# One-hot tiles for 256 tokens: two broadcast compares and a GpSimd multiply, or eight scalar compares per four tokens

## The reference

```python
def peer(h, w_q, sub_k1, sub_k2, u, v):
    ...
    sc, pos = lax.top_k(cand, PEER_TOPK)                 # 16 experts for each of 8 heads
    eidx = jnp.take_along_axis(cidx, pos, axis=-1)       # expert number = i1 * 128 + i2
    gate = jax.nn.softmax(sc, axis=-1)
    ...
        act = jax.nn.gelu(jnp.einsum('td,thkd->thk', hx, u[ex]))
        return jnp.einsum('thk,thkd->td', (gx.astype(act.dtype) * act), v[ex])
```

## Time and profile before

| | |
|---|---|
| median of 3 runs | 1987.02 us (1985.88 to 1988.28) |
| the profiled execution, device time | 1985.47 us |
| its span, first to last instruction | 1983.6 us |
| busy: TensorE, its weight loads | 1738.9 us (88%), 1106.4 us (56%) |
| busy: VectorE | 1137.5 us (57%) |
| busy: ScalarE | 244.2 us (12%) |
| busy: GpSimd | 694.1 us (35%) |
| mean granted TensorE clock | 0.934 of full |
| DMA | 475.53 MB, mean 240 GB/s |

### The profile page before, as it was taken

One profiled execution on the slowest core, in us unless ns is written; L12 is line 12 of the kernel. 1 busy time (PEld: TensorE's weight loads), 2 busy tenths in 40 slices (PEclk: granted clock), 3 DMA queues, 4 the chain that ended last, 5 costly groups with the idle time before them and its releaser, 6 DMA issues.

```text
span 1983.6 us, 17251 instructions
## 1 busy us (share of the span) xinstructions
PE 1738.9 (88%) x6170; PEld 1106.4 (56%) x6170; DVE 1137.5 (57%) x2433; ACT 244.2 (12%) x601; POOL 694.1 (35%) x714
## 2 busy tenths in 40 slices
PE   6979899999999899999999993768999999995067
PEld 3454344333678588888888882655444444442033
DVE  0011233333120999999974568999565555668933
ACT  2002232233011102111111110000000000000023
POOL 0001133333000233333443446776444333546700
PEclk9979899999999999999999996778999999998589
DMA  5231110100544579999998997114999999999911
GB/s 199 74 117 54 32 33 21 30 2 2 189 139 149 191 280 339 367 370 362 364 384 323 409 409 288 58 53 172 409 409 409 409 409 409 409 409 404 409 49 43
DMA packets 131969, 475.53 MB, mean 240 GB/s; under 512 B 14715, under 2 KB 15739, under 8 KB 131884
## 3 DMA queue, kind: packets, MB, share of 16 engines
q0 software_dynamic: 73728, 268.47, 35.1%
q1 hardware_dynamic: 58156, 205.97, 28.1%
HBM read 471.19 MB, written 3.19 MB: 239 GB/s over the span
## 4 chain that ended last, share of the span: by engine, by line
PE 55%; DMA 27%; DVE 9%; POOL 4%; issue 4%; ACT 1%; SPq 0%; DVEq 0%; ACTq 0%; POOLq 0%
DMA arena<-in_v,eidx 19%; PE psum L1366 16%; DMA arena<-in_u,eidx 7%; PE psum L1215 6%; PE psum L1277 6%; PE psum L1113 5%; POOL arena L477 4%; PE psum L1193 3%; PE psum L1237 3%; PE psum L1326 3%; PE psum L1249 3%; PE psum L1377 3%; PE psum L1165 2%; DVE arena L973 2%; DVE arena L951 2%
## 5 line engine op out<-in xcount | busy, mean ns | idle before, releaser
L1366 PE MATMUL psum<-arena 128*128 128x256 f32 x2048 | 442.5, 379 | 0.7 <-ACT arena L589 0.7
L1384 PE MATMUL psum<-arena 128*128 128x512 f32 x1024 | 440.4, 592 | 2.8 <-DMA arena<-in_vd 2.0
L477 POOL DMA_INDIRECT arena<-in_u,eidx x256 | 246.9, 964 | 518.2 <-DVE dots L951 293.3
L973 DVE SCALAR_TENSOR_TENSOR arena<-arena,wts 128x1024 f32<-128x1024 f32 x254 | 325.7, 1285 | 169.6 <-DMA arena<-in_v,eidx 169.5
L1366 PEld LDWEIGHTS psum<-arena 128*128 128x128 f32 x2048 | 389.0, 190 | 53.7 <-ACT arena L589 0.9
L951 DVE CUSTOM_DVE_ANT_0 arena<-psum,arena 128x1024 f32<-128x1024 f32 x256 | 304.0, 1222 | 64.4 <-DMA arena<-in_u,eidx 62.3
L477 POOL DMA_INDIRECT arena<-in_v,eidx x256 | 249.8, 976 | 253.7 <-DVE arena L973 219.5
L1384 PEld LDWEIGHTS psum<-arena 128*128 128x128 f32 x1024 | 194.2, 190 | 247.7 <-issue 243.0
L458 POOL TENSOR_SCALAR arena<-arena 128x256 f32<-128x256 f32 (+4 forms) x128 | 105.9, 846 | 375.6 <-DVE arena L747 245.1
L1377 PE MATMUL psum<-arena 128*128 128x128 f32 x512 | 103.2, 366 | 71.5 <-POOL arena L487 28.9
L1377 PEld LDWEIGHTS psum<-arena 128*128 128x128 f32 x512 | 90.5, 266 | 84.5 <-issue 43.4
(11 more groups left out here) (167 smaller groups left out, 1348.3 us busy)
## 6 DMA issues: line engine op xcount, KB each, us to landing
arena<-in_ut SPq DMA_DIRECT2D x128, 512.0 KB, 6.8
arena<-in_vd SPq DMA_DIRECT2D x128, 512.0 KB, 6.8
arena<-in_wpack SPq DMA_DIRECT2D x105, 512.0 KB, 3.7
arena<-in_u,eidx POOLq DMA_INDIRECT x256, 8.9
arena<-in_v,eidx POOLq DMA_INDIRECT x256, 14.7
arena<-in_w_pg SPq DMA_DIRECT2D x8, 512.0 KB, 8.9
arena<-in_x SPq DMA_DIRECT2D x4, 512.0 KB, 4.8
arena<-bias_rows SPq DMA_DIRECT2D x8, 256.0 KB, 5.4
```

The source lines that it names most:

```text
L477: G.indirect_dma_start(out=slots[n % SLOTS], out_offset=None, in_=a["v"] if values else a["u"], in_offset=bass.IndirectOffsetOnAxis(ap=eid ...
L973: V.scalar_tensor_tensor(to, row, w, to, ALU.mult, ALU.add).then_inc(row_used, 1)
L1366: last = T.matmul(ps[6 + c % 2][:, 0:DT], u[:, k * P:(k + 1) * P], h2T1[:, k, :], start=(k == 0), stop=(k == KC - 1))
L1384: last = T.matmul(ps[BANK + 2 * t + h], mixed[:, c, t * P:(t + 1) * P], stream[:, c % SRING, h * HALF:(h + 1) * HALF], start=(c == 0), sto ...
```

## The change

`make_hots` makes each token's one-hot by itself, with tensor_scalar instructions of 128x128: `iota` is compared with a per-partition scalar, a column of `pickT`. For `hot2` a second operation of the same instruction multiplies by the gate, a second per-partition scalar. Four such instructions are made for `hot2` and four for `hot1`, and the semaphore goes up with the last of each four. The multiply on GpSimd, its two waits and the semaphore `hot2_gated` are gone; GpSimd's gathers stay in their order. TensorE waits for `hot2_ready`.

```diff
@@ gpsimd
             for n in range(before):
                 gather(n)
-            pool.wait_ge(picks_out, 2)
             for g in range(WG):
-                pool.wait_ge(hot2_ready, g + 1)
-                G.tensor_tensor(hot2[:, g % 2, :, :], hot2[:, g % 2, :, :],
-                                pickT[:, 2, WGRP * g:WGRP * (g + 1)].unsqueeze(2).broadcast_to([P, WGRP, P]),
-                                ALU.mult).then_inc(hot2_gated, 1)
                 if g % W_STEP == W_STEP - 1 and g // W_STEP >= 1:
                     gather(before + g // W_STEP - 1)
@@ vector
             def make_hots(g):
                 if g >= 2:
                     dve.wait_ge(mix_made, g - 1)
-                V.tensor_tensor(hot2[:, g % 2, :, :], iota[:, :].unsqueeze(1).broadcast_to([P, WGRP, P]),
-                                pickT[:, 1, WGRP * g:WGRP * (g + 1)].unsqueeze(2).broadcast_to([P, WGRP, P]),
-                                ALU.is_equal).then_inc(hot2_ready, 1)
-                V.tensor_tensor(hot1[:, g % 2, :, :], iota[:, :].unsqueeze(1).broadcast_to([P, WGRP, P]),
-                                pickT[:, 0, WGRP * g:WGRP * (g + 1)].unsqueeze(2).broadcast_to([P, WGRP, P]),
-                                ALU.is_equal).then_inc(hot1_ready, 1)
+                for j in range(WGRP):
+                    tok = WGRP * g + j
+                    last = V.tensor_scalar(hot2[:, g % 2, j, :], iota[:, :], pickT[:, 1, tok:tok + 1],
+                                           pickT[:, 2, tok:tok + 1], ALU.is_equal, ALU.mult)
+                last.then_inc(hot2_ready, 1)
+                for j in range(WGRP):
+                    tok = WGRP * g + j
+                    last = V.tensor_scalar(hot1[:, g % 2, j, :], iota[:, :], pickT[:, 0, tok:tok + 1], None, ALU.is_equal)
+                last.then_inc(hot1_ready, 1)
@@ tensor
             for g in range(WG):
                 pe.wait_ge(hot1_ready, g + 1)
-                pe.wait_ge(hot2_gated, g + 1)
+                pe.wait_ge(hot2_ready, g + 1)
```

More of the change, by code:

```diff
@@ L299, in build @@
         hot2_ready = sem("hot2_ready")
-        hot2_gated = sem("hot2_gated")
         mix_made = sem("mix_made")
```

## The result

The changed kernel takes 2008.53 us (median of 3 runs, 2003.60 to 2012.12) against 1987.02 before: +21.5 us between the medians. The ratio of the runs on record is 1.0099, with a 95% interval of 1.0069 to 1.0129. It is slower, as forecast, by over three times what I forecast (+6.4). The number lies within 0.1 us of the first rival's, the second scalar that costs as much as the first (2008.6).

The account below looks back on a forecast made before the run. VectorE was taken to bound the one-hot stage: 140.3 + 18.2 = 158.5 us against 152.1, so +6.4. With everything behind the stage unchanged, 1987.0 + 6.4 = 1993.4 us; range 1988 to 2013.

Parts of the forecast that it names:

- first rival: hot2 instructions in the one-hot stage: second fetched scalar costs another 0.06 us, 0.259 each; +21.6 us, 2008.6; chance 0.27.
- What bounds the stage: Loop over 64 four-token groups, 152.1 us: VectorE sets the pace, TensorE close behind; mean period 2.38 us.
- the 133.4 us of VectorE: Stage before the change: VectorE's need if nothing held it, 64 x (0.60 + 0.60 + 0.60) + 16 x 1.14.
- The coupling: DMA-bound stretch behind the stage stays as long: a microsecond of the stage is a microsecond of the end.
- Part (a): GpSimd's 64 multiplies go, and with them the hold on L1006 (7 us) and late matmuls (up to 9.6 us).
- Part (c): Eight tensor_scalar of 128x128 per group at 0.199 us each, second scalar free: 1.59 us per group against 1.20.
- the slow rate: Sign in the changed trace that comparing isn't done at two elements per step: starts 0.26 us apart.
- Part (e): TensorE in the stage: matmuls take at most 2.06 us plus 0.3, within 2.79 us, so VectorE's waits for them vanish.
- the case that I had given 0.42: The forecast itself: second scalar's fetch costs nothing more, stage 158.5 us, +6.4 us, time 1993.4 us.
- The hidden fetch: One-hot instructions: fetch hidden when short, 0.139 us each; TensorE last, stage 134 us, -18, time 1969; chance 0.13.
- the slow comparison: One-hot instructions: is_equal not at two elements per step, 0.266 us each; +41 us, 2028, or 2043; chance 0.07.
- A lock for a gather's whole length: Stage's 16 GpSimd gathers each stop VectorE for 0.94 us: 15 us on top of the forecast, 2008.5; chance 0.05.

Follow-up runs that it names:

- per-token version: Kernel before with the gate multiply moved from GpSimd to ScalarE and a semaphore raised for each token: 2039.21 us beside 2054.80 for the kernel before, on a disturbed chip.
- half change: Changed kernel with hot1 made by the one broadcast comparison of before, hot2 still by four tensor_scalar: 2006.96 us, ratio 1.0098; later 2071.16 and 2066.52 us on disturbed chips.

## Why the prediction was right or wrong

**What bounds the stage** held. VectorE's instructions from start to start give the length of every stage, and without the multiply the 133.4 us of VectorE became 135.0.

**The coupling** held in all kernels: the rest is 611.9 to 614.4 us for stages of 128 to 174 us, begun anywhere from 1217 to 1293. Where the stage began on time, its difference is the kernel's. For the change that is 174.4 - 152.1 = +22.3 of a span that grew by 23.1; it began 2.4 us later and its rest was 1.6 shorter.

**Part (a)**, what GpSimd's leaving gives, held: 7 + 9.6 reckoned, 17.1 measured.

**Part (c)** held for the first scalar: 0.199 us reckoned, 0.197 measured, at two elements per step with is_equal as well. It failed at the second scalar. I gave it the lower end, nothing, "the two come from one row of the same tile, and nothing in the rows says that the fetch is longer than its latency". The measured term is 0.06 us on each of 256 instructions, 15.4 us, beside a miss of 15.1 (2008.5 against 1993.4). The stage without it was 16.5 us shorter, since the 1.5 us beside the gathers went with it. Nothing in the rows spoke for the overlap either. They showed that not even the next instruction's start hides a fetch, and the nearest priced thing to a second fetch was the first. The hot2 starts of 0.256 us also look like the 0.26 that I had named as the sign of the slow rate. It is not that: the hot1 starts are at 0.197, and with no fetch the same comparison and multiply take 0.136.

**Part (e)** held: 0.5 us of waits for matmuls remain.

**The rivals.** The second scalar is what happened, and its time came out to 0.1 us of the median. The mechanism is shown, but so close a hit is luck: the three runs spread over 8.5 us, and the rival had neither the 1.5 us beside the gathers nor the later start of 2.4. My range held only because it took in this rival; the case that I had given 0.42 did not come. The hidden fetch and the slow comparison are ruled out by the starts. The page's 58 cycles of fixed cost (the Trainium skill, VectorE: DVE Perf Modes, The TRN2 errata) do fit where no scalar is fetched: the estimate of 127 ns from that page stands beside 136 measured. With one and two fetches the instruction is 70 and 129 ns over the page. That rival's time, 1969, had a second fault, TensorE at the lower clock level throughout: with no fetch the kernel took 1961.24.

In the changed kernel the groups beside a gather lose a little, 0.09 us each and 1.5 us in all, where I had put nothing or 15. With one fetched scalar in each comparison, or none, they lose nothing; why it takes the second one stays open. A lock for a gather's whole length would have cost 0.94 each time, so the exclusion for a whole instruction of which the Trainium skill speaks (SBUF — State Buffer, Who interferes with whom) is not seen here for gathers.

## What to carry to other kernels

Price an instruction by its start-to-start time and count its fetched scalars one by one: here 0.136 us at 128x128, and 0.06 more for each. A broadcast comparison of 128x512 (0.60 us) beats four of 128x128 with one scalar (0.79), even though those run at twice the rate. Folding a helper engine's step into the engine that sets the pace can cost more than the helper's interference: look first for an engine that is idle in that stage and does not hold it up.

## What the runs showed of the hardware that I had not expected

Two scalars from the very same address cost as much as two from different ones (1.03 us for four). The second operation of a tensor_scalar is free here (is_equal, then mult: 0.79 us for four with one operation and with two).

The disturbance goes with the split of the DMA between two queues. The DMA queues between 1060 and 1180 us (packets, MB, share of 16 engines), first in the kernel before as profiled, then in the per-token version:

```profile
q0 software_dynamic: 8113, 29.57, 62.4%
q1 hardware_dynamic: 4874, 17.74, 37.7%
```

```profile
q0 software_dynamic: 11771, 42.89, 90.8%
q1 hardware_dynamic: 1158, 4.19, 9.0%
```

Both move some 47 MB in this time. In the second, GpSimd's gathers (q0) take nine tenths, the streamed blocks that TensorE needs (q1) get the rest, and the scores end 92 us later. The blocks were asked for in time: SyncE waited 109.5 of these 120 us for a matmul to free a place of its ring in the first, and 3.1 in the second (27.4 more for something that the trace does not name). The half change whose stage began 14 us late lies between, with 33.0 MB for q0 and 12.8 for q1. The edits are not the cause: six of the seven times of the kernel before on that chip are 2050 to 2075 us, though no trace of them is kept. What tips the split was not tried and stays open.
